# One weight part instead of two is cut between the second gated product and its transposed halves

## The chip, the cores and the metric

The kernel runs on one core of one Trainium2 chip. The metric is the device time of one execution in microseconds, from the first to the last instruction and what lies around them. Of the runs before, the median of three counts.

## What is computed

One decoder layer over 2048 tokens of width 1024: a token mixer with pooling and windowed attention, and then a mixture of experts. The change lies in the experts. Cut to them, the reference is:

```python
def _hier_moe(h, w_group_router, b_group_router, w_expert_router, b_expert_router,
              w_gate, w_up, w_down):
...
    def run_block(args):
        tok, e = args
        xb = h[tok]
        a = xb @ w_gate[e]
        u = xb @ w_up[e]
        return (jax.nn.silu(a) * u) @ w_down[e]

    y = lax.map(run_block, (slot_tok.reshape(n_blocks, MOE_BLOCK), block_expert))
    y = y.reshape(n_slots, D_MODEL) * slot_w[:, None]
    return jnp.zeros((t_count, D_MODEL), h.dtype).at[slot_tok].add(y)
```

Each token goes to 2 of 32 experts; an expert has a gate and an up matrix of 1024x512 and a down matrix of 512x1024, all in float32. The tokens of an expert are padded to blocks of 128.

## The kernel before

The stages follow each other: normalise, project, attend, merge, mix_out, route, experts, combine. The function `experts` runs over blocks of 128 tokens. A row of `table` tells of each block which expert it has, and whether that is a new one. Blocks are sorted by expert; a block whose *next* block has a new expert is called a reload block here. In this case 48 blocks run.

**Precision.** Every float32 matrix is split into a high part (a copy in fp32r) and a low part (the rest): ScalarE makes the high part, VectorE subtracts it to get the low part, and TensorE multiplies three times: high by high, high by low, low by high (`three`, lines 1585 to 1587). To split a part of the weights is called a cut: `cut_high` (L1507, ACT) and `cut_low` (L1513, DVE).

**Weights.** An expert is 12 parts of 512 KB: parts 0 to 3 are the gate and up columns of the first half (256 columns each), 4 to 7 those of the second half, 8 to 11 the down matrix. SyncE loads a raw part (L1214, L1217) when the low cut of the part before it in the same buffer is done (`lo_ready`). There is one raw buffer, and one pair of high and low buffers. So the weights of the next expert are cut within a reload block, each part after its last use in that block (`used[g]`), and the raw parts of the expert behind it are loaded meanwhile.

**A block on TensorE**, in program order: `gate_up(0, 0..3)`, turn (transpose) the gathered tokens of the next block (`turn_x`, L1576), `gate_up(1, 0)`, `gate_up(1, 1)`, turn half 0 of the gated product (`turn_h(0)`), `gate_up(1, 2)`, `gate_up(1, 3)`, `down(0)`, `turn_h(1)`, `down(1)`, wait for `lo_taken[1]`, `down(2)`, `down(3)`. The wait is for the low part of the turned half 1, `moe_hT_lo`. A `down(k)` is six matmuls of 512 columns.

**The same block on ScalarE and VectorE.** ScalarE: `silu(0)` (L1660), high part of the turned tokens (L1639), cuts, high part of turned half 0, cuts, `silu(1)`, cuts, high part of turned half 1 (`take_h(1)`, `moe_hT_hi`), cuts, and last the scaled output (`moe_ys`, L1676). VectorE does the same with `multiply` (L1715), the low parts (L1694) and `cut_low`. The cuts are under a branch that is taken in reload blocks alone. The order on each engine is written out by hand in these functions; each waits for semaphores of the others:

```python
                def take_low(half, dst, hi, n_tiles, count):
                    dve.wait_ge(hi_taken[half], count)
                    dve.tensor_tensor(dst, p_turn[:, half, 0:n_tiles * P], hi, ALU.subtract).then_inc(lo_taken[half], 1)
```

**GpSimd** gathers the tokens of block b+2 (`moe_xg`, L1546) and then adds the output of block b to the sum in memory by an indirect DMA (L1555); the next gather is issued when that scatter has landed.

Of the kernel before, what the change touches and what calls it, by code (L numbers as in the profile page):

```python
# [1223 lines left out]
GU, PARTS = 8, 12  # L1224
# [224 lines left out]
def experts(nc, table, slot_rows, slot_place, slot_share, ident, h_dram, raw_gu, raw_d, w_gate, w_up, w_down, y_sum, x1_dram):  # L1449
# [5 lines left out]
    with ExitStack() as ctx:  # L1455
# [26 lines left out]
        def entry(eng, r, b, top):  # L1482
            return eng.value_load(table[0:1, r, ds(b, 1)], min_val=0, max_val=top)

        def by_twos(eng, body):

            count = entry(eng, 3, 0, NB)
            with eng.Fori(0, NB // 2) as i:
                with eng.If(2 * i < count):
                    body(i)  # L1490
            return count
# [10 lines left out]
        def cut_high(act, g, n, b):  # L1502

            act.wait_ge(part_loaded[g], (32 if g < GU else 16) * n)
            if b is not None:
                act.wait_ge(used[g], b + 1)
            nc.scalar.activation(hi_part(g), raw_part(g), ACT.Copy).then_inc(hi_ready[g], 1)  # L1507

        def cut_low(dve, g, n, b):
            dve.wait_ge(hi_ready[g], n)  # L1510
            if b is not None:
                dve.wait_ge(used[g], b + 1)
            dve.tensor_tensor(lo_part(g), raw_part(g), hi_part(g), ALU.subtract).then_inc(lo_ready[g], 1)  # L1513

        with nc.Block() as block:
            @block.sync
            def _(sp):
                def load(e, before):

                    for g in range(PARTS):  # L1520
                        sp.wait_ge(lo_ready[g], before)
                        load_part(sp, g, e, raw_gu, raw_d, w_gate, w_up, w_down, part_loaded[g])

                for g in range(PARTS):
                    sp.sem_inc(part_loaded[g], 32 if g < GU else 16)  # L1525

                def reload(b):
                    with sp.If(entry(sp, 1, b, 1) > 0):
                        load(entry(sp, 0, b, NE - 1), entry(sp, 2, b, NE))

                by_twos(sp, lambda i: [reload(2 * i), reload(2 * i + 1)])

                cut = entry(sp, 2, NB, NE) + 1
                for g in range(PARTS):
                    sp.wait_ge(lo_ready[g], cut)
                    sp.dma_start(x1_part(g, raw_gu, raw_d), x1_dram[ds(g * P, P), :]).then_inc(x1_loaded, 16)
                sp.wait_ge(x1_loaded, 16 * PARTS)
# [99 lines left out]
            @block.scalar  # L1637
            def _(act):
                copy = lambda dst, src: nc.scalar.activation(dst, src, ACT.Copy)  # L1639

                def take_high(half, dst, n_tiles, count):
                    act.wait_ge(turned[half], count + (4 if half else 0))
                    copy(dst, p_turn[:, half, 0:n_tiles * P]).then_inc(hi_taken[half], 1)

                def take_x(u, count):
                    for half in range(2):
                        take_high(half, xT_hi[:, u, ds(4 * half, 4), :].rearrange("p k c -> p (k c)"), 4, count)

                def block_of(b, u):
                    new = entry(act, 1, b + 1, 1)  # L1650
                    n = entry(act, 2, b + 1, NE) + 1

                    def cuts(parts):
                        with act.If(new > 0):
                            for g in parts:
                                cut_high(act, g, n, b)

                    def silu(half):
                        act.wait_ge(used[4 * half + 3], b + 1)
                        nc.scalar.activation(act_g[:, half, :], p_gu[:, half, 0, 0:H2], ACT.Silu).then_inc(silu_ready[half], 1)  # L1660

                    def take_h(half):
                        take_high(half, hT_hi[:, ds(2 * half, 2), :].rearrange("p k c -> p (k c)"), 2, 2 * b + 3)

                    silu(0)
                    take_x(1 - u, 2 * b + 2)
                    cuts(range(0, 2))
                    take_h(0)
                    cuts(range(2, 3))
                    silu(1)  # L1670
                    cuts(range(3, 5))
                    take_h(1)
                    cuts(range(5, PARTS))
                    act.wait_ge(used[PARTS - 1], b + 1)
                    act.wait_ge(scattered, b + 1)
                    nc.scalar.activation(ys[:, u, :], p_y[:, :, :].rearrange("p a c -> p (a c)"), ACT.Copy,  # L1676
                                         scale=slot_share[:, ds(b, 1)]).then_inc(y_ready, 1)

                for g in range(PARTS):
                    cut_high(act, g, 1, None)  # L1680
                    if g == 1:
                        take_x(0, 1)
                by_twos(act, lambda i: [block_of(2 * i, 0), block_of(2 * i + 1, 1)])

            @block.vector
            def _(dve):
                dve.sem_inc(y_ready, 1)
                for u in range(2):
                    dve.sem_inc(hid_ready[u], 1)
                    dve.sem_inc(lo_taken[u], 1)  # L1690
# [5 lines that stand above are left out]
                def flat(t, k, n):  # L1696
                    return t[:, ds(k, n), :].rearrange("p k c -> p (k c)")

                def take_x(u, count):
                    for half in range(2):  # L1700
                        take_low(half, flat(xT_lo[:, u, :, :], 4 * half, 4), flat(xT_hi[:, u, :, :], 4 * half, 4), 4, count)

                def block_of(b, u):
                    new = entry(dve, 1, b + 1, 1)
                    n = entry(dve, 2, b + 1, NE) + 1

                    def cuts(parts):
                        with dve.If(new > 0):
                            for g in parts:
                                cut_low(dve, g, n, b)  # L1710

                    def multiply(half):
                        dve.wait_ge(silu_ready[half], b + 1)
                        dve.wait_ge(used[4 * half + 3], b + 1)
                        dve.tensor_tensor(hid[:, half, :], p_gu[:, half, 1, 0:H2], act_g[:, half, :], ALU.mult  # L1715
                                          ).then_inc(hid_ready[half], 1)

                    def take_h(half):
                        take_low(half, flat(hT_lo, 2 * half, 2), flat(hT_hi, 2 * half, 2), 2, 2 * b + 3)

                    multiply(0)
                    take_x(1 - u, 2 * b + 2)
                    cuts(range(0, 2))
                    take_h(0)
                    cuts(range(2, 3))
                    multiply(1)
                    cuts(range(3, 5))
                    take_h(1)
                    cuts(range(5, PARTS))

                for g in range(PARTS):
                    cut_low(dve, g, 1, None)
                    if g == 1:
                        take_x(0, 1)
                by_twos(dve, lambda i: [block_of(2 * i, 0), block_of(2 * i + 1, 1)])


# [130 lines left out]
```

## Time and profile before

| | |
|---|---|
| median of 3 runs | 2729.76 us (2728.51 to 2739.48) |
| profiled execution | 2733.67 us, span 2731.9 us, mean granted TensorE clock 0.946 |
| PE busy | 2381.6 us (87%) |
| DVE, ACT, POOL busy | 1338.9, 933.1, 549.2 us |
| blocks run (moe_ys) | 48, from 1767.8 to 2659.9 us |
| loads of an expert | 16 of 256 KB and 4 of 512 KB |

Engines are PE (TensorE; PEld its weight loads), ACT (ScalarE), DVE (VectorE), POOL (GpSimd), SP (SyncE). The expert stage is roughly the stretch from 1752 to 2660 us; the combine stage behind it ends the program. Busy time of PE contains overlapping matmuls: a matmul of 512 columns takes 0.39 us, and one starts each 0.235 us.

### The profile page before, as it was taken

What the parts mean: (1) busy time and instruction counts of PE and PEld (TensorE: products, weight loads), DVE (VectorE), ACT (ScalarE), POOL (GpSimd) and SP (SyncE); (2) the same over time, 40 slices, a digit from 0 to 9 for tenths busy, and PEclk for the clock granted to TensorE, in tenths of its full rate; (3) what the DMA queues carried; (4) which work ended last, traced back from release to release, by engine and by line L of the source; (5) the groups of instructions that cost most, each with busy time, mean ns of one, the idle gap of its engine ahead of it and who ended that gap; (6) DMA issues with size and microseconds to landing.
All of it is one profiled execution on the core that took longest, in us unless ns stands there. A gap on an engine that the chain in (4) does not pass through costs nothing. (4 is left out here: it accounts for less than half of the span.)

```text
span 2731.9 us, 39222 instructions
## 1 busy us (share of the span) xinstructions
PE 2381.6 (87%) x13485; PEld 2039.5 (75%) x13486; DVE 1338.9 (49%) x1673; ACT 933.1 (34%) x1541; POOL 549.2 (20%) x375
## 2 busy tenths in 40 slices
PE   3599999999999968876969995699999999999990
PEld 3488888888888857764857884588898988988880
DVE  7552111123232257636534445888666384655536
ACT  3200000000000035533322221587666375655533
POOL 2311111111111020002334552222222222212220
PEclk9999999999999989957989996799999999999995
DMA  6123222223424233226555444599999597878847
GB/s 231 46 77 123 90 95 98 86 104 111 138 92 138 107 122 119 92 98 216 212 185 195 155 155 153 186 353 356 320 305 284 137 353 231 282 217 279 246 146 292
DMA packets 291435, 493.43 MB, mean 181 GB/s; under 512 B 21145, under 2 KB 226481, under 8 KB 281778
## 3 DMA queue, kind: packets, MB, share of 16 engines
q1 hardware_dynamic: 272658, 424.53, 44.9%
q0 software_dynamic: 14112, 51.39, 8.0%
q10 hardware_dynamic: 4608, 16.78, 1.5%
q8 instruction: 32, 0.52, 0.1%
q14 instruction: 25, 0.20, 0.0%
HBM read 374.98 MB, written 117.64 MB: 180 GB/s over the span
## 5 line engine op out<-in xcount | busy, mean ns | idle before, releaser
L357 PE MATMUL proj_psum<-h_hi,proj_w_hi 128*128 128x512 f32 x1216 | 481.7, 396 | 19.0 <-POOL proj_w_lo L342 19.0
L359 PE MATMUL proj_psum<-h_hi,proj_w_lo 128*128 128x512 f32 x1216 | 481.4, 396 | 0.0
L358 PE MATMUL proj_psum<-h_lo,proj_w_hi 128*128 128x512 f32 x1216 | 481.4, 396 | 0.0
L1585 PE MATMUL moe_p_gu<-moe_hi_gu,moe_xT_hi 128*128 128x256 f32 x1536 | 437.4, 285 | 1.7 <-DVE moe_xT_lo L1694 1.7
L378 DVE COPY proj_out<-proj_psum 128x512 f32<-128x512 f32 x152 | 123.7, 815 | 634.4 <-PE proj_psum L359 633.3
L1586 PE MATMUL moe_p_gu<-moe_lo_gu,moe_xT_hi 128*128 128x256 f32 x1536 | 428.7, 279 | 0.0
L1587 PE MATMUL moe_p_gu<-moe_hi_gu,moe_xT_lo 128*128 128x256 f32 x1536 | 428.6, 279 | 0.0
L1513 DVE TENSOR_TENSOR moe_lo_gu<-raw_gu,moe_hi_gu 128x1024 fp32r<-128x1024 f32 x256 | 302.1, 1220 | 23.5 <-ACT moe_hi_gu L1507 19.4
L335 ACT ACTIVATE proj_w_hi<-proj_raw 128x1024 fp32r<-128x1024 f32 x38 | 40.4, 1062 | 781.5 <-PE proj_psum L359 748.0
L1586 PEld LDWEIGHTS moe_p_gu<-moe_lo_gu,moe_xT_hi 128*128 128x128 f32 x1536 | 291.1, 190 | 2.1
L1585 PEld LDWEIGHTS moe_p_gu<-moe_hi_gu,moe_xT_hi 128*128 128x128 f32 x1536 | 289.2, 188 | 4.2 <-issue 2.1
L1587 PEld LDWEIGHTS moe_p_gu<-moe_hi_gu,moe_xT_lo 128*128 128x128 f32 x1536 | 290.4, 189 | 0.0
L357 PEld LDWEIGHTS proj_psum<-h_hi,proj_w_hi 128*128 128x128 f32 x1216 | 228.8, 188 | 74.6 <-issue 19.3
L359 PEld LDWEIGHTS proj_psum<-h_hi,proj_w_lo 128*128 128x128 f32 x1216 | 228.7, 188 | 55.6
L358 PEld LDWEIGHTS proj_psum<-h_lo,proj_w_hi 128*128 128x128 f32 x1216 | 228.8, 188 | 55.3
L1507 ACT ACTIVATE moe_hi_gu<-raw_gu 128x1024 fp32r<-128x1024 f32 x256 | 256.9, 1056 | 14.3 <-SPq L1525 11.3
L342 POOL TENSOR_TENSOR proj_w_lo<-proj_raw,proj_w_hi 128x1024 fp32r<-128x1024 f32 x38 | 97.8, 2575 | 724.6 <-ACT proj_w_hi L335 724.6
L1585 PE MATMUL moe_p_y<-moe_hi_d,moe_hT_hi 128*128 128x512 f32 x384 | 159.2, 415 | 34.4 <-DVE moe_hT_lo L1694 34.2
L1555 POOL DMA_INDIRECT y_sum<-moe_ys,moe_place x48 | 99.6, 2075 | 345.6 <-ACT moe_ys L1676 334.5
L1715 DVE TENSOR_TENSOR moe_hid<-moe_p_gu,moe_act_g 128x256 f32<-128x256 f32 x96 | 40.7, 424 | 245.8 <-ACT moe_act_g L1660 242.1
L1587 PE MATMUL moe_p_y<-moe_hi_d,moe_hT_lo 128*128 128x512 f32 x384 | 151.9, 396 | 0.0
L1586 PE MATMUL moe_p_y<-moe_lo_d,moe_hT_hi 128*128 128x512 f32 x384 | 151.8, 395 | 0.0
(268 smaller groups left out, 3772.0 us busy)
## 6 DMA issues: line engine op xcount, KB each, us to landing
raw_gu<-in_w_exp_gate SPq DMA_DIRECT2D x256, 256.0 KB, 5.8
raw_gu<-in_w_exp_up SPq DMA_DIRECT2D x256, 256.0 KB, 5.9
raw_d<-in_w_exp_down SPq DMA_DIRECT2D x128, 512.0 KB, 7.9
projected<-proj_out SPq DMA_DIRECT2D x38, 1024.0 KB, 3.9
proj_raw<-in_w_in SPq DMA_DIRECT2D x38, 512.0 KB
att_qkv<-projected SPq DMA_DIRECT2D x18, 1024.0 KB
proj_w_rest<-in_w_ada SPq DMA_DIRECT2D x8, 2048.0 KB
merge_gate<-projected SPq DMA_DIRECT2D x32, 512.0 KB, 5.0
```

The source lines that it names most:

```text
L342: pool.tensor_tensor(w_lo[:, u, :, :], raw[:, u, :, :], w_hi[:, u, :, :], ALU.subtract).then_inc(lo_ready[u], 1)
L357: pe.matmul(bank, w_hi[:, u, k, :], h_hi[:, k, tok], start=(k == 0), stop=False)
L358: pe.matmul(bank, w_hi[:, u, k, :], h_lo[:, k, tok], start=False, stop=False)
L359: mm = pe.matmul(bank, w_lo[:, u, k, :], h_hi[:, k, tok], start=False, stop=(k == KD - 1))
L378: ins = dve.tensor_copy(view[:, ds(tg * per, per), :], psum[:, u, tg, :].rearrange("p (m r) -> p m r", r=dilation))
L1507: nc.scalar.activation(hi_part(g), raw_part(g), ACT.Copy).then_inc(hi_ready[g], 1)
L1513: dve.tensor_tensor(lo_part(g), raw_part(g), hi_part(g), ALU.subtract).then_inc(lo_ready[g], 1)
L1555: pool.indirect_dma_start(out=y_sum, out_offset=bass.IndirectOffsetOnAxis(ap=place[:, u:u + 1], axis=0), in_=ys[:, u, :], in_offset=None, ...
L1585: pe.matmul(bank, x_hi, w_hi, start=first, stop=False)
L1586: pe.matmul(bank, x_hi, w_lo, start=False, stop=False)
L1587: return pe.matmul(bank, x_lo, w_hi, start=False, stop=last)
L1715: dve.tensor_tensor(hid[:, half, :], p_gu[:, half, 1, 0:H2], act_g[:, half, :], ALU.mult).then_inc(hid_ready[half], 1)
```

## The change

On ScalarE and on VectorE, the list of parts that are cut between the second gated product (`silu(1)`, `multiply(1)`) and the copies of its turned half (`take_h(1)`) holds part 3 alone instead of parts 3 and 4. Part 4 is cut first behind those copies. No instruction is added or taken away.

```diff
@@ experts, ACT
                     take_h(0)
                     cuts(range(2, 3))
                     silu(1)
-                    cuts(range(3, 5))
+                    cuts(range(3, 4))
                     take_h(1)
-                    cuts(range(5, PARTS))
+                    cuts(range(4, PARTS))
                     act.wait_ge(used[PARTS - 1], b + 1)
                     act.wait_ge(scattered, b + 1)
@@ experts, DVE
                     take_h(0)
                     cuts(range(2, 3))
                     multiply(1)
-                    cuts(range(3, 5))
+                    cuts(range(3, 4))
                     take_h(1)
-                    cuts(range(5, PARTS))
+                    cuts(range(4, PARTS))
```

On VectorE, in a block's second part, from the branch before the cuts to the end of the block (moe_lo_gu is the low part of gate/up weights, moe_lo_d of down weights, moe_hT_lo of the turned product):

```order
-L1513 TENSOR_TENSOR moe_lo_gu<-raw_gu,moe_hi_gu 128x1024 x2
+L1513 TENSOR_TENSOR moe_lo_gu<-raw_gu,moe_hi_gu 128x1024
 L1708 UNCONDITIONAL_BRANCH
 L1694 TENSOR_TENSOR moe_hT_lo<-moe_p_turn,moe_hT_hi 128x256
 L1708 COMPARE_AND_BRANCH
 L1510 REGISTER_ALU
-L1513 TENSOR_TENSOR moe_lo_gu<-raw_gu,moe_hi_gu 128x1024 x3
+L1513 TENSOR_TENSOR moe_lo_gu<-raw_gu,moe_hi_gu 128x1024 x4
 L1513 TENSOR_TENSOR moe_lo_d<-raw_d,moe_hi_d 128x1024 x4
 L1708 UNCONDITIONAL_BRANCH
```

One low cut has moved from ahead of moe_hT_lo to behind it; the order of the cuts among themselves is the same.

On ScalarE, the same place (moe_hi_gu and moe_hi_d are high parts of the weights, moe_hT_hi of the turned product):

```order
-L1507 ACTIVATE moe_hi_gu<-raw_gu 128x1024 x2
+L1507 ACTIVATE moe_hi_gu<-raw_gu 128x1024
 L1654 UNCONDITIONAL_BRANCH
```

and in the changed kernel from there on:

```order
L1507 ACTIVATE moe_hi_gu<-raw_gu 128x1024
L1654 UNCONDITIONAL_BRANCH
L1642 REGISTER_ALU
L1639 ACTIVATE moe_hT_hi<-moe_p_turn 128x256
L1654 COMPARE_AND_BRANCH
L1504 ISA
L1507 ACTIVATE moe_hi_gu<-raw_gu 128x1024 x4
L1504 REGISTER_ALU
L1507 ACTIVATE moe_hi_d<-raw_d 128x1024 x4
```

One high cut stands ahead of moe_hT_hi and eight behind it, where there were two and seven. TensorE, GpSimd and SyncE have the same instructions in the same order.

## Rows read from the trace of the kernel before

**Rows 1.** Windows: busy us (instructions) of PE, PEld, DVE, ACT, POOL; clock, DMA share, GB/s

```profile
1752.00:1912.00 160.00, 149.16 (x1070) 136.31 (x1069) 136.77 (x147) 126.96 (x158) 35.39 (x29) 1.00 1.07 356
...
2195.00:2253.00 58.00, 54.63 (x394) 50.17 (x393) 50.11 (x54) 47.00 (x59) 13.66 (x13) 1.00 1.07 353
...
1752.00:2660.00 908.00, 868.82 (x6274) 801.66 (x6272) 571.57 (x663) 556.17 (x732) 197.07 (x188) 1.00 0.87 273
```

**Rows 2.** Waits of PE, 1752 to 1928: total us, times, longest

```profile
PE moe_p_y L1585 <- DVE moe_hT_lo L1694: 8.4, 8, 1.1
```

**Rows 3.** Waits of PE, 1928 to 2665

```profile
PE moe_p_y L1585 <- DVE moe_hT_lo L1694: 25.9, 23, 1.1
```

**Rows 4.** The page's groups: busy us, mean ns, idle before

```profile
L1507 ACT ACTIVATE moe_hi_gu<-raw_gu 128x1024 fp32r<-128x1024 f32 x256 | 256.9, 1056 | 14.3 <-SPq L1525 11.3
```

**Rows 5.** Timeline of ACT in a reload block: start us, us, instruction

```profile
2032.23 0.39 ACT L1660 ACTIVATE moe_act_g<-moe_p_gu 128x256 f32<-128x256 f32 x1 [1.50 <-PE moe_p_gu L1587]
2032.51 2.00 ACT L1507 ACTIVATE moe_hi_gu<-raw_gu 128x1024 fp32r<-128x1024 f32 x2
2034.40 0.37 ACT L1639 ACTIVATE moe_hT_hi<-moe_p_turn 128x256 fp32r<-128x256 f32 x1
2034.67 2.95 ACT L1507 ACTIVATE moe_hi_gu<-raw_gu 128x1024 fp32r<-128x1024 f32 x3
```

**Rows 6.** Timeline of DVE in the same block and up to the next

```profile
2025.99 0.42 DVE L1715 TENSOR_TENSOR moe_hid<-moe_p_gu,moe_act_g 128x256 f32<-128x256 f32 x1 [9.23 <-ACT moe_act_g L1660]
...
2032.64 0.42 DVE L1715 TENSOR_TENSOR moe_hid<-moe_p_gu,moe_act_g 128x256 f32<-128x256 f32 x1 [0.65 <-ACT moe_act_g L1660]
2033.59 2.36 DVE L1513 TENSOR_TENSOR moe_lo_gu<-raw_gu,moe_hi_gu 128x1024 fp32r<-128x1024 f32 x2 [0.52 <-ACT moe_hi_gu L1507]
2035.87 0.42 DVE L1694 TENSOR_TENSOR moe_hT_lo<-moe_p_turn,moe_hT_hi 128x256 fp32r<-128x256 f32 x1
2036.20 3.49 DVE L1513 TENSOR_TENSOR moe_lo_gu<-raw_gu,moe_hi_gu 128x1024 fp32r<-128x1024 f32 x3
2039.61 4.62 DVE L1513 TENSOR_TENSOR moe_lo_d<-raw_d,moe_hi_d 128x1024 fp32r<-128x1024 f32 x4
2045.52 0.42 DVE L1715 TENSOR_TENSOR moe_hid<-moe_p_gu,moe_act_g 128x256 f32<-128x256 f32 x1 [1.28 <-ACT moe_act_g L1660]
```

**Rows 7.** Timeline of PE in the same block

```profile
2033.43 0.38 PE L1576 MATMUL moe_p_turn<-ident,moe_hid 128*128 128x128 f32 x2
...
2034.82 0.40 PE L1587 MATMUL moe_p_y<-moe_hi_d,moe_hT_lo 128*128 128x512 f32 x1
2036.34 0.50 PE L1585 MATMUL moe_p_y<-moe_hi_d,moe_hT_hi 128*128 128x512 f32 x1 [1.12 <-DVE moe_hT_lo L1694]
```

**Rows 8.** Waits of ACT, 1752 to 1912

```profile
ACT moe_hi_d L1507 <- DMA raw_d<-in_w_exp_down: 5.5, 13, 1.4
```

**Rows 9.** Timeline of ACT, 1838 to 1849

```profile
1845.70 1.06 ACT L1507 ACTIVATE moe_hi_d<-raw_d 128x1024 fp32r<-128x1024 f32 x1 [0.52 <-DMA raw_d<-in_w_exp_down]
```

**Rows 10.** Timeline of ACT in a block without a reload

```profile
2071.09 0.39 ACT L1660 ACTIVATE moe_act_g<-moe_p_gu 128x256 f32<-128x256 f32 x1 [2.44 <-PE moe_p_gu L1587]
2072.72 0.39 ACT L1639 ACTIVATE moe_hT_hi<-moe_p_turn 128x256 fp32r<-128x256 f32 x1 [1.24 <-PE moe_p_turn L1576]
```

**Rows 11.** Timeline of POOL: two gathers

```profile
1999.32 1.49 POOL L1546 DMA_INDIRECT moe_xg<-h_moe,moe_row  x1 [0.81 <-POOL moe_row L1543]
...
2224.45 1.16 POOL L1546 DMA_INDIRECT moe_xg<-h_moe,moe_row  x1 [0.81 <-POOL moe_row L1543]
```

**Rows 12.** Tile moe_xg, the same two gathers: issue to landing, in this order

```profile
DMA to landing us min/median/max: 7.7/7.7/7.7
...
DMA to landing us min/median/max: 7.3/7.3/7.3
```

**Rows 13.** Timeline of PE: the turns of these two gathers' tokens

```profile
2007.42 1.03 PE L1576 MATMUL moe_p_turn<-ident,moe_xg 128*128 128x128 f32 x8
...
2233.47 1.04 PE L1576 MATMUL moe_p_turn<-ident,moe_xg 128*128 128x128 f32 x8
```

## The prediction

> **What bounds the kernel now.** The change touches only the expert stage, so I first asked which engine sets its pace. In its 908 us TensorE is busy 868.8 us at a granted clock of 1.00, while VectorE has 572 us and ScalarE 556 us [rows 1]. So TensorE is the bound wherever nothing holds it up, and I read next what does. In the lists of TensorE's waits one entry stands out: its down product (moe_p_y) waits for VectorE's low part of the transposed product (moe_hT_lo), 8 times for 8.4 us up to 1928 us [rows 2] and 23 times for 25.9 us after it [rows 3]. That is 31 times 1.1 us, and 31 is the number of reload blocks: 48 blocks run, and 256 high cuts of gate/up parts [rows 4], eight to an expert, are 32 experts, of which the first is cut ahead of the loop. The wait exists only where the cuts stand between, so it belongs to the edited place.
>
> One reload block shows the order. ScalarE starts the second silu at 2032.23, makes two high cuts from 2032.51 and only then copies the transposed high part at 2034.40 [rows 5]. VectorE starts its two low cuts at 2033.59 and hT_lo at 2035.87 [rows 6]. TensorE has ended the two transposes at 2033.81, runs the last matmul of down(1) from 2034.82 and starts down(2) at 2036.34, idle for 1.12 us [rows 7]. The reader is to see that the transposes were done well ahead of both copies: what is late is VectorE.
>
> The second thing to see is the DMA. From 1752 to 1912 us, eight reload blocks in a row, the DMA share is 1.07 at 356 GB/s; it is the same in 2195 to 2253, and 0.87 over the stage [rows 1]. In the first run ScalarE waits 13 times for a down part to land [rows 8], for the first time at 1845.70, in the fifth block [rows 9]; after 1912 us its list has no such wait.
>
> **The change part by part.** Nothing is added: 12 high and 12 low cuts per reload block stay. Part 4 moves behind the copy of the transposed half 1.
>
> *VectorE.* Two low cuts and the step to hT_lo take 2035.87 - 2033.59 = 2.28 us [rows 6], so 1.14 each. With one cut, hT_lo may start at 2034.73 if its high part is there. That copy needs the transposes' end at 2033.81 [rows 7]; counted from the second silu, a block without cuts has it at 2072.72 - 2071.09 = 1.63 us [rows 10], here 2033.86, while the one high cut left ends at about 2033.5. The copy takes 0.37 and ends at 2034.25, 0.5 us before VectorE asks. So VectorE's part 3 remains the last to end, and the gain is one cut, 1.14 us.
>
> *TensorE.* It started down(2) 0.47 us behind hT_lo's start, so now at 2035.20. Its own pace is 0.235 per matmul, so it was free at 2034.82 + 0.235 = 2035.06 [rows 7]. A wait of 0.14 us is left; it could at most have won 1.28. Gain: 1.14 per reload block.
>
> *What moves later.* ScalarE now stands idle from 2033.5 to 2033.86 in front of the transposes, with all remaining cuts queued behind. Part 5 was cut from 2034.67 [rows 5]; now part 4 starts at about 2034.13 and part 5 at 2035.1, 0.4 us later. On VectorE part 4 starts at about 2035.2 and part 5 at 2036.35, against 2036.20 [rows 6]: 0.15 later. VectorE ends its last cut (started in the group at 2039.61, 4 x 1.14) near 2044.4 instead of 2044.23, and is wanted for the next multiply at 2045.52 - 1.14 = 2044.38 [rows 6]. So its idle 1.28 us shrinks to nothing, just without a loss. ScalarE keeps about 1 us. A few tenths late there are covered: turn_h(0) comes only after two more gate/up parts. If the cover were gone, the 0.15 to 0.4 us per block would be paid.
>
> *Loads.* SyncE issues a raw part once its low cut is done. An expert is 6.29 MB, a gather and a scatter 0.52 MB each: 7.34 MB per reload block, at 355 GB/s (between the two runs' rates) 20.7 us. A reload block has 2045.52 - 2025.99 = 19.5 us, of which the row at 2045.52 is the second end. The DMA already needs more than the blocks give it. In the first run the lead is used up, and its end is set by the landings: what TensorE wins there it loses again. So for the 8 blocks ahead of 1928 us I take 0, from bounds of 0 and 8 x 1.14 = 9.1 us. Later runs are at most four blocks; the deficit grows from 1.2 to 2.3 us per block. The first run lost its lead, some 5 us, within five blocks [rows 9]; three intervals now cost 6.9, so the last block of the two runs of four could see its down parts up to 1.9 us late, mostly hidden by ScalarE's slack: 0 taken, 3.8 as a bound.
>
> *Gathers.* A gather is issued only when the scatter of three blocks before has landed, which does not move with the stall of the block between. The gather at 1999.32 landed 7.7 us later, at 2007.0 [rows 11, 12], and its tokens were turned at 2007.42 [rows 13]: 0.4 us of slack against 1.14. This one costs 0.7. The one at 2224.45 landed at 2231.75 and was wanted at 2233.47: 1.7 of slack, 0.6 left. VectorE's cuts show 11 places after 1928 us where two reload blocks follow each other, and so 11 gathers of this kind. I let 2 of the other 10 slip like the first (0.9 each): 0.7 + 1.8 = 2.5 us; bounds 0.7 and 0.7 + 9.
>
> The DMA limit is where a page speaks. The row shows 356 GB/s at a share of 1.07 with ScalarE waiting for landings. The Trainium skill, page "DMA: Bandwidth & Descriptors", section "Measured (HBM→SBUF, 128 partitions, SWDGE, issued from GpSimd)", has 425 GB/s for a core whose neighbour is idle. By that figure an expert's block would need 17.3 us, no run would be held, and the first rival below would be right. The trace does not agree: at a full share it moves 356 over 160 us, and I go by the row.
>
> **Sum.** 23 x 1.14 = 26.2, less 2.5, is 23.7 us. The profiled execution took 2733.67 us with a span of 2731.9; it becomes 2710.0. The median of the runs is 2729.76, 0.14% below it, and becomes 2706.1. I predict 2706. What follows the experts starts with the last block's end and moves as a whole.
>
> **The rivals.**
> *Full gain in all 31 blocks.* If the first run were paced by TensorE after all, 31 x 1.14 = 35.3 us go: 2694.4. For it: that run's first four blocks show no landing wait. Against: the 13 waits behind them [rows 8]. 7%.
> *The DMA takes more.* All 10 close gathers slip by 0.9 and both runs of four end 1.9 late: 26.2 - 9.7 - 3.8 = 12.7 us gained, 2717. For it: the share of 1.07 in 2195 to 2253 already now [rows 1], and gathers pass through the same engines. Against: four later blocks with it show no wait for a landing. 14%.
> *No change.* VectorE is so full that the next multiply and x copies are late by what was won, or the wait merely turns into one for the next x: about 2730. For it: 1.28 us of idle time against 1.14 + 0.15. Against: it still waits 0.65 us for the second silu [rows 6], which takes up a few tenths just ahead of the place that matters. 8%.
> *Slower.* ScalarE's stand in front of the transposes becomes the pace: cuts, low cuts and reloads all come 0.4 us later per reload block, and TensorE waits for the parts instead: 31 x 0.4 = 12.4 us, 2742. It decides where the transposes end more than 0.5 us after part 3's high cut and VectorE has no idle time left. Against: they end 0.3 after it. 3%.
> My forecast has the remaining 68%, with a range of its own of 2700 to 2712.
>
> **The numbers.** About 0.5%, 13.6 us, is what a measurement here tells from no change, so "faster" begins under 2716.1. The forecast, the full gain and nearly half of the DMA rival lie there: 0.68 + 0.07 + 0.07 = 0.82; slower by over 0.5% (above 2743.4) is half of its rival and stray cases: 0.03; the same 0.15. The range is 2698 to 2718: it takes in the forecast and nearly all of the DMA rival, and leaves out the full gain, no change and slower.
>
> **What would show it.** TensorE's wait for moe_hT_lo falls from 1.1 to 0.1 to 0.2 us, the start of down(2) stands 0.47 behind hT_lo; ScalarE idles about 0.3 before that copy. Blocks with a reload take 18.4 us instead of 19.5, those without stay at 17.9. Before 1928 us nothing is won and ScalarE waits longer for raw_d. New waits of TensorE for moe_xg appear, the first near 2007. VectorE's idle time before the multiply after a reload block is close to 0. The prediction is wrong if the first run also gets shorter, if waits for moe_xg come in most runs, or if ScalarE's waits for landings appear after 1928 us.

## The result and the profile after

The changed kernel took 2716.05 us (median of 6 runs, 2713.35 to 2722.47); the kernel before 2733.89 (6 runs, 2728.51 to 2739.48). The ratio is 0.9937, interval 0.992 to 0.9955: 17 us faster, between 12 and 22. The prediction had 23.7 us less and 2706; its range, 2698 to 2718, holds the time near its upper end. Of the 10 us between 2706 and 2716, 4 are there because the forecast counted from 2729.76, the median of three runs of the kernel before, and all six have 2733.89; the other 6 are a smaller gain. One execution of all those below, at 3167.91 us and a granted clock of 0.728 beside 0.93 to 0.95 in the others, is left out of every median and ratio.

The profiled execution took 2717.12 us, its span is 2715.4. The same block as in [rows 5 to 7], a reload block after one without, in the timeline of the changed kernel; TensorE first:

```profile
2033.27 0.38 PE L1576 MATMUL moe_p_turn<-ident,moe_hid 128*128 128x128 f32 x2
...
2034.65 0.40 PE L1587 MATMUL moe_p_y<-moe_hi_d,moe_hT_lo 128*128 128x512 f32 x1
2035.04 0.50 PE L1585 MATMUL moe_p_y<-moe_hi_d,moe_hT_hi 128*128 128x512 f32 x1
```

ScalarE:

```profile
2025.39 0.38 ACT L1660 ACTIVATE moe_act_g<-moe_p_gu 128x256 f32<-128x256 f32 x1 [2.30 <-PE moe_p_gu L1587]
...
2032.06 0.38 ACT L1660 ACTIVATE moe_act_g<-moe_p_gu 128x256 f32<-128x256 f32 x1 [1.50 <-PE moe_p_gu L1587]
2032.34 1.05 ACT L1507 ACTIVATE moe_hi_gu<-raw_gu 128x1024 fp32r<-128x1024 f32 x1
2033.68 0.38 ACT L1639 ACTIVATE moe_hT_hi<-moe_p_turn 128x256 fp32r<-128x256 f32 x1 [0.29 <-PE moe_p_turn L1576]
2033.96 3.89 ACT L1507 ACTIVATE moe_hi_gu<-raw_gu 128x1024 fp32r<-128x1024 f32 x4
2037.75 3.89 ACT L1507 ACTIVATE moe_hi_d<-raw_d 128x1024 fp32r<-128x1024 f32 x4
2041.55 1.10 ACT L1676 ACTIVATE moe_ys<-moe_p_y,slot_share 128x1024 f32<-128x1024 f32 x1
```

VectorE:

```profile
2033.42 1.23 DVE L1513 TENSOR_TENSOR moe_lo_gu<-raw_gu,moe_hi_gu 128x1024 fp32r<-128x1024 f32 x1 [0.52 <-ACT moe_hi_gu L1507]
2034.57 0.42 DVE L1694 TENSOR_TENSOR moe_hT_lo<-moe_p_turn,moe_hT_hi 128x256 fp32r<-128x256 f32 x1
2035.05 4.63 DVE L1513 TENSOR_TENSOR moe_lo_gu<-raw_gu,moe_hi_gu 128x1024 fp32r<-128x1024 f32 x4
2039.60 4.62 DVE L1513 TENSOR_TENSOR moe_lo_d<-raw_d,moe_hi_d 128x1024 fp32r<-128x1024 f32 x4
2044.14 0.41 DVE L1715 TENSOR_TENSOR moe_hid<-moe_p_gu,moe_act_g 128x256 f32<-128x256 f32 x1
```

The step between the two matmuls of TensorE is 0.39 us, where it was 1.52. hT_lo starts 2.51 us behind the second silu instead of 3.64, ScalarE stands 0.29 us in front of the transposes, and the next multiply follows VectorE's last cut without idle time. So far each row is as foreseen, but for 0.1 us: the multiply starts 0.54 us behind its silu at 2043.60, where it was 0.42. Now what TensorE waits for, in two lists of its waits, 1752 to 1930 and 1930 to 2650 us, which answer to [rows 2, 3]:

```profile
PE moe_p_turn L1576 <- DMA moe_xg<-h_moe,moe_row: 6.6, 5, 2.0
PE moe_p_turn L1576 <- DVE moe_xT_lo L1694: 4.2, 3, 2.1
PE moe_p_y L1585 <- DVE moe_hT_lo L1694: 0.3, 1, 0.3
```

```profile
PE moe_p_turn L1576 <- DMA moe_xg<-h_moe,moe_row: 9.2, 10, 1.9
```

The wait for moe_hT_lo is gone, and one for the gathered tokens, moe_xg, has come: 9.2 us behind the first run, in place of 25.9. Nine of its ten waits, 8.4 us, stand in the 11 places where two reload blocks have just followed each other; the tenth, 0.8 us, is in the tenth block, where the kernel before waited 1.3. Reading the same two marks in every trace, the first silu of the tenth block and the last moe_ys, gives the table that the experiments below are read by. "First run" is from the first silu to the tenth block's, "rest" from there to the start of the last moe_ys; both in us. The stage begins at another time in each trace (1737.7 to 1764.6), by differences ahead of it; the two stretches leave that out, and what lies behind them takes 71.8 to 72.4 us in all.

| kernel | first run | rest | both |
|---|---|---|---|
| before | 175.2 | 731.7 | 907.0 |
| changed | 176.4 | 713.4 | 889.8 |
| VectorE's list alone | 175.7 | 713.8 | 889.6 |
| ScalarE's list alone | 177.5 | 742.3 | 919.8 |
| changed, gather ahead | 177.2 | 704.4 | 881.6 |
| before, gather ahead | 176.2 | 729.6 | 905.8 |
| before, half loads | 173.3 | 730.9 | 904.2 |
| changed, half loads | 163.4 | 703.9 | 867.3 |
| changed, moe_ys early | 175.9 | 701.7 | 877.6 |
| before, moe_ys early | 177.2 | 729.8 | 907.0 |
| no part between | 176.5 | 728.2 | 904.7 |
| changed, both cures | 176.4 | 702.6 | 879.0 |

Each row is one execution. The change won 18.3 us in the rest and lost 1.2 in the first run; the three versions of the kernel before with full loads have 175.2 to 177.2 there, so 1.2 is no more than they differ among themselves.

### The profile page after: what moved, and what is told of

Read it like the earlier page. It is cut to its first block and busy times, and to the rows that moved or that the text cites. A ratio compares the mean times of both kernels' runs of the same rounds, so it can differ in the third digit from the quotient of the medians.

```text
span 2715.4 us, 39222 instructions
## 1 busy us (share of the span) xinstructions
PE 2385.7 (88%) x13485; PEld 2043.5 (75%) x13486; DVE 1337.3 (49%) x1673; ACT 935.4 (34%) x1541; POOL 534.0 (20%) x375
## 5 line engine op out<-in xcount | busy, mean ns | idle before, releaser
L1555 POOL DMA_INDIRECT y_sum<-moe_ys,moe_place x48 | 93.0, 1937 | 343.5 <-ACT moe_ys L1676 330.9
L1513 DVE TENSOR_TENSOR moe_lo_d<-raw_d,moe_hi_d 128x1024 fp32r<-128x1024 f32 x128 | 148.8, 1217 | 4.6 <-ACT moe_hi_d L1507 4.2
```

The lines of the kernel that those rows point to most:

```text
L1555: pool.indirect_dma_start(out=y_sum, out_offset=bass.IndirectOffsetOnAxis(ap=place[:, u:u + 1], axis=0), in_=ys[:, u, :], in_offset=None, ...
```

## Why the gathers came due

My theory after the result: a gather is released by the landing of the scatter three blocks before, that scatter by moe_ys, and moe_ys stands on ScalarE behind the cuts. TensorE's gain did not move moe_ys forward within its block at all. In the block shown it starts 2041.55 - 2025.39 = 16.16 us behind the first silu. Before it was

```profile
2041.30 1.11 ACT L1676 ACTIVATE moe_ys<-moe_p_y,slot_share 128x1024 f32<-128x1024 f32 x1
```

(timeline of ACT), 15.73 us behind the silu at 2025.57. So it became 0.43 us later within the block, while TensorE became 1.14 earlier in this block and again in the next. One close gather of the changed kernel, from ScalarE's timeline, GpSimd's and TensorE's:

```profile
2188.75 1.10 ACT L1676 ACTIVATE moe_ys<-moe_p_y,slot_share 128x1024 f32<-128x1024 f32 x1
...
2190.67 2.22 POOL L1555 DMA_INDIRECT y_sum<-moe_ys,moe_place  x1 [11.61 <-ACT moe_ys L1676]
2200.75 0.97 POOL L1543 COPY moe_row<-slot_rows 128x1 int32 x1 [7.85 <-DMA y_sum<-moe_ys,moe_place]
2202.51 1.17 POOL L1546 DMA_INDIRECT moe_xg<-h_moe,moe_row  x1 [0.80 <-POOL moe_row L1543]
...
2208.87 0.28 PE L1587 MATMUL moe_p_gu<-moe_hi_gu,moe_xT_lo 128*128 128x256 f32 x1
2209.78 0.66 PE L1576 MATMUL moe_p_turn<-ident,moe_xg 128*128 128x128 f32 x4 [0.62 <-DMA moe_xg<-h_moe,moe_row]
```

From moe_ys to the turn there are 21.0 us, of which the chain takes all. The reader should follow the brackets backwards: TensorE waits for the gather, the gather's row copy for the scatter's landing, the scatter for moe_ys. The rivals were that VectorE, now full, takes the time, and that the loads do.

## The experiments

Each ratio is to executions of the kernel before that lie beside those of the experiment. Their median is 2732.74 us for the lists of one engine and the gathers, 2737.43 for the half loads, the early output on the changed kernel and no part between, and 2737.49 for the two that remain. So across these groups only ratios and the two stretches are compared, not times.

**One engine's list alone.** Each leaves the other engine as before.

```diff
 # VectorE alone: block_of of the vector engine
-                    cuts(range(3, 5))
+                    cuts(range(3, 4))
                     take_h(1)
-                    cuts(range(5, PARTS))
+                    cuts(range(4, PARTS))
```

> Only VectorE's list is changed (part 3 alone ahead of moe_hT_lo); ScalarE keeps parts 3 and 4 ahead of moe_hT_hi. Theory (the won time is lost at gathers, which hang on the scaled output moe_ys; moe_ys is queued on ScalarE behind the cuts and came 0.4 us later with the change): TensorE's wait for moe_hT_lo goes as it did with the change (0.1 to 0.2 us left), moe_ys stays at 15.75 us behind the block's first silu instead of 16.15, and TensorE's waits for moe_xg after 1930 us fall from 9.2 us to 4 to 6. Time 3 to 5 us below the changed kernel's, ratio to before 0.992 to 0.993. Rival (VectorE is full, its late multiply costs the time): waits and time as with the change, ratio 0.9937.

Measured: 2717.2 us, ratio 0.9943 (0.9925 to 0.9961). The gain is VectorE's, as both theories had it. The further 3 to 5 us did not come, and this expectation missed: moe_ys did return to 15.7 us, but the waits fell only to 7.5 us, not to 4 to 6:

```profile
PE moe_p_turn L1576 <- DMA moe_xg<-h_moe,moe_row: 7.5, 10, 1.0
```

The scatter of the same block as above, in GpSimd's timeline, shows where the 0.4 us went:

```profile
2190.22 2.55 POOL L1555 DMA_INDIRECT y_sum<-moe_ys,moe_place  x1 [11.21 <-ACT moe_ys L1676]
2200.76 1.12 POOL L1543 COPY moe_row<-slot_rows 128x1 int32 x1 [7.99 <-DMA y_sum<-moe_ys,moe_place]
```

It is issued 0.45 us earlier, takes 2.55 instead of 2.22 us and has landed at the same time. A shift this small doesn't tell the theories apart.

> Only ScalarE's list is changed; VectorE keeps parts 3 and 4 ahead of moe_hT_lo. Theory: VectorE's second low cut is what holds TensorE, so the wait of 1.1 us stays in all 31 reload blocks, while moe_ys comes about 0.4 us later: ratio 1.000 to 1.002. Rival (ScalarE's high cut is what is late): the wait falls to under 0.5 us and the ratio to 0.995.

Measured: 2747.33 us, ratio 1.0056 (1.0038 to 1.0074), 15 us slower than before. I had missed that VectorE's second low cut needs the high cut of the same part, and that this now stands behind the wait for the transposes. ScalarE, then VectorE, in a reload block:

```profile
2034.44 0.38 ACT L1660 ACTIVATE moe_act_g<-moe_p_gu 128x256 f32<-128x256 f32 x1 [1.50 <-PE moe_p_gu L1587]
...
2036.34 3.89 ACT L1507 ACTIVATE moe_hi_gu<-raw_gu 128x1024 fp32r<-128x1024 f32 x4
...
2037.43 1.22 DVE L1513 TENSOR_TENSOR moe_lo_gu<-raw_gu,moe_hi_gu 128x1024 fp32r<-128x1024 f32 x1 [0.40 <-ACT moe_hi_gu L1507]
2038.57 0.42 DVE L1694 TENSOR_TENSOR moe_hT_lo<-moe_p_turn,moe_hT_hi 128x256 fp32r<-128x256 f32 x1
```

hT_lo starts 4.13 us behind the silu instead of 3.64. TensorE's 23 waits in the rest are 37.1 us, 1.6 each, against 25.9. TensorE has no wait for the gathers in this stretch; its reload blocks are slower than before.

**The gather ahead of the scatter's landing**, on the changed kernel and on the one before. Besides what is shown, the row table and its zeroed tail get two more columns, as gathers now run one block further ahead.

```diff
...
+                def landed(b):
                     pool.wait_ge(added, 16 * b + 16)
                     pool.sem_inc(scattered, 1)
 
                 def block_of(b, u):
-                    gather(b + 2, u)
                     scatter(b, u)
+                    gather(b + 3, 1 - u)
+                    landed(b)
...
                 gather(1, 1)
+                gather(2, 0)
```

> The changed kernel, with GpSimd issuing the gather for block b+3 right behind the scatter of block b instead of after that scatter has landed (its own wait for the landing comes behind the gather). Theory: no wait of TensorE for moe_xg is left after 1930 us (9.2 us now), so reload blocks there take 18.4 us each and 23 x 1.14 = 26 us are won against before in that stretch, while the first run up to 1930 us stays held by the loads: 2706 to 2709, ratio 0.990 to 0.991. Rival (the loads or VectorE take the time and the gathers' waits only stand where another would): the waits move elsewhere and the ratio stays 0.993 to 0.994.

> The kernel before with the same earlier gathers, as the control. Theory: its gathers had 0.4 us of slack or more except two (2.1 us of waits), so 0 to 2 us are won: ratio 0.999 to 1.000. Rival (gathers behind the scatters were a cost of the kernel before as well): ratio 0.996 or less.

Measured: the changed kernel with it 2710.76 us, ratio 0.9928 (0.99 to 0.9955); the one before with it 2730.65, ratio 0.9993 (0.9983 to 1.0003). The ratio is above the 0.990 to 0.991 expected and hardly below the rival's 0.993, and the four times lie between 2703.62 and 2716.62, which is more than the effect. By the times alone nothing is decided; the traces decide: the rest is 704.4 us against 713.4, and the list of TensorE's waits in it is empty. Against before that is 27.3 us. In the kernel before, the same edit brought 2.1 us in the rest. The first run did not get shorter with either.

**Half of the bytes of each reload**, before and changed. The other half of each raw part keeps the first expert's values, so these two kernels do not compute the reference's result; they serve to see what the loads cost.

```diff
+            eng.dma_start(raw_gu[:, g, m, 0, :], w[0, ds(e, 1), ds(kp * 2 * P, P), ds(half * H2, H2)]
+                          .rearrange("e p f -> p (e f)")).then_inc(loaded, 16)
...
+        eng.dma_start(raw_d[:, g - GU, 0:D // 2], w_down[0, ds(e, 1), ds((g - GU) * P, P), 0:D // 2].rearrange("e p f -> p (e f)")
```

> The kernel before, with each reload of an expert's part fetching only half of its bytes (one of two row groups of gate/up, half the columns of down); the rest of the raw part keeps the first expert's values, so what the experts compute is not the reference's. Theory: the loads bound the kernel before only at the end of its first run of reload blocks, so little changes: first run up to the tenth block about 1 us shorter, the rest 0 to 2 us; ratio 0.998 to 1.000. Rival (loads slow the whole stage through the DMA engines): ratio under 0.995.

> The changed kernel with the same halved reloads (the same part of the computation altered). Theory: with the DMA engines at little more than half their load neither landings nor gathers hold the blocks, so all 31 reload blocks keep the 1.14 us: 35 us against the halved kernel before, 2695 to 2699, ratio to before 0.986 to 0.988; first run about 9 us shorter than before's 175.2. Rival A (the first run is held by something else): the first run stays at 175 to 176 us, ratio 0.990. Rival B (VectorE is full and takes part of it): waits on neither, yet the reload blocks take 18.8 us or more.

Measured: 2729.19 us, ratio 0.9973 (0.9954 to 0.9992), and 2690.68, ratio 0.9835 (0.9815 to 0.9855): 38.5 us between the two. The kernel before hardly noticed the halved loads, 1.9 us in the first run and 0.8 in the rest. The changed one did: its first run fell from 176.4 to 163.4 us, 9.9 below the halved kernel before. All 31 blocks now keep what they won: 904.2 - 867.3 = 36.9 us in the two stretches. ScalarE's waits in the first run say what it was. In the changed kernel they were

```profile
ACT moe_hi_d L1507 <- DMA raw_d<-in_w_exp_down: 7.5, 16, 1.3
...
ACT moe_hi_gu L1507 <- DMA raw_gu<-in_w_exp_up: 4.7, 8, 1.3
```

and with half loads neither is in the list. The windows of 160 us over the first run, changed kernel and then half loads:

```profile
1752.00:1912.00 160.00, 150.97 (x1073) 137.81 (x1072) 137.11 (x147) 126.68 (x157) 28.86 (x28) 0.99 1.07 356
```

```profile
1765.00:1925.00 160.00, 158.73 (x1141) 145.52 (x1140) 137.50 (x152) 127.75 (x162) 36.97 (x33) 1.00 0.78 216
```

TensorE is busy for 158.7 of 160 us once the DMA share is 0.78. It is also seen that VectorE, with as much work as ever (137.1 and 137.5 us), was not what held the blocks. The edit takes both effects away at once: the landing of a gather, 7.1 us in the median in the kernel before, is 5.1 here, and no wait for moe_xg is left in the rest. As issuing the gather earlier removes the same wait with the loads whole, the wait needs both, the late issue and the loads beside it.

**moe_ys ahead of the last three high cuts**, on the changed kernel and on the one before.

```diff
-                    cuts(range(4, PARTS))
+                    cuts(range(4, 9))
                     act.wait_ge(used[PARTS - 1], b + 1)
                     act.wait_ge(scattered, b + 1)
                     nc.scalar.activation(ys[:, u, :], ...
+                    cuts(range(9, PARTS))
```

> The changed kernel, with ScalarE's scaled output moe_ys put ahead of the last three high cuts instead of behind them (it comes 2.5 to 3 us earlier in the block). Theory (the gathers hang on moe_ys through the landing of the scatter): TensorE's waits for moe_xg after 1930 us fall from 9.2 us to under 2, and the stretch behind the first run takes 705 to 707 us instead of 713.4: 2708 to 2710, ratio 0.991. Rival (the scatter's landing is set by the loads queued in the DMA engines, not by its issue): the waits stay at 6 to 9 us and the ratio at 0.994.

> The kernel before (two parts ahead of the transposed halves), with moe_ys ahead of the last three high cuts. Control for the last run but one: if the gathers had slack before, the earlier output wins next to nothing there: PE's waits for moe_hT_lo stay at 34 us, the stretch behind the first run at 729 to 731 us, ratio 0.998 to 1.000. Rival (the earlier output helps by itself, whatever the gathers): ratio 0.995 or less.

Measured: 2703.08 us, ratio 0.9887 (0.9865 to 0.991), on the changed kernel, and 2735.85, ratio 1.0 (0.9983 to 1.0017), on the one before. ScalarE's timeline shows the output between the cuts of the down parts:

```profile
2030.24 1.05 ACT L1507 ACTIVATE moe_hi_d<-raw_d 128x1024 fp32r<-128x1024 f32 x1
2031.19 1.10 ACT L1676 ACTIVATE moe_ys<-moe_p_y,slot_share 128x1024 f32<-128x1024 f32 x1
2032.19 2.95 ACT L1507 ACTIVATE moe_hi_d<-raw_d 128x1024 fp32r<-128x1024 f32 x3
```

With the output 2.9 us earlier, the list of TensorE's waits in the rest is empty, and the rest is 701.7 us, 3 us below what was expected. The loads and GpSimd's own order are as in the changed kernel, so the late output is what released the gathers late. This is the fastest version with whole loads: 1.1% below before, and by the ratios 0.5% below the changed kernel. The same edit without the change wins nothing: the gathers had slack there.

**No part between**, on both engines.

```diff
-                    cuts(range(3, 4))
                     take_h(1)
-                    cuts(range(4, PARTS))
+                    cuts(range(3, PARTS))
```

> No part at all is cut between the second gated product and its transposed halves, on both engines. Theory: the last 0.15 us of TensorE's wait for moe_hT_lo goes, but VectorE then stands idle until the high part is there and has 1.0 us of cuts more behind it than there is room for; its multiply and copies come late in runs of reload blocks and moe_ys about 1 us later still, so the gathers' waits grow to 15 to 20 us: 2720 to 2730, ratio 0.995 to 0.999. Rival (the cuts behind are hidden): ratio 0.992 to 0.994.

Measured: 2731.24 us, ratio 0.9986 (0.997 to 1.0002), 1 us over the time foreseen, within the ratio. The rest of the stage is 728.2 us. TensorE's waits in 1925 to 2700, then ScalarE and VectorE around the end of a reload block that another one precedes:

```profile
PE moe_p_turn L1576 <- DMA moe_xg<-h_moe,moe_row: 20.2, 9, 2.5
```

```profile
2057.99 1.09 ACT L1675 ACTIVATE moe_ys<-moe_p_y,slot_share 128x1024 f32<-128x1024 f32 x1
2059.10 1.28 ACT L1660 ACT_TABLE_LOAD   x1
2060.39 0.38 ACT L1660 ACTIVATE moe_act_g<-moe_p_gu 128x256 f32<-128x256 f32 x1
```

```profile
2050.54 5.77 DVE L1513 TENSOR_TENSOR moe_lo_gu<-raw_gu,moe_hi_gu 128x1024 fp32r<-128x1024 f32 x5 [0.53 <-ACT moe_hi_gu L1507]
2056.22 4.62 DVE L1513 TENSOR_TENSOR moe_lo_d<-raw_d,moe_hi_d 128x1024 fp32r<-128x1024 f32 x4
2060.81 0.42 DVE L1714 TENSOR_TENSOR moe_hid<-moe_p_gu,moe_act_g 128x256 f32<-128x256 f32 x1
```

The multiply starts 0.42 us behind its silu in a free block, and here too, 2060.81 with a silu at 2060.39: VectorE is not what is late, because the silu is late too, behind moe_ys and the load of a function table (ACT_TABLE_LOAD, 1.28 us). One part between is thus the best of the three as the rest of the kernel stands: with two VectorE holds TensorE, with none ScalarE's output and the gathers do. No part between together with the early output was not tried.

**Both cures together.**

> The changed kernel with both cures, the gather ahead of the scatter's landing and moe_ys ahead of the last three high cuts. Theory: both remove the same waits, so together they give what one gives: no wait for moe_xg, the stretch behind the first run at 701 to 705 us, the first run held by the loads at 175 to 177 us; ratio 0.988 to 0.990. Rival (the two cure different losses): the stretch falls below 700 us, ratio 0.986 or less.

Measured: 2707.42 us, the median of three runs (2702.9 to 2714.63), ratio 0.9892 (0.9844 to 0.9941). The rest is 702.6 us, beside 704.4 and 701.7 with one cure. They remove the same waits.

## Why the prediction was right, and where it was off

The wait, the size of what it gives back and the hold of the loads on the first run were foreseen for the right reasons. The loss to the gathers was named, but priced at a quarter of what it was. By one of its own signs the prediction was wrong there: it said so of waits for moe_xg that come in most runs, and they come in all seven runs of two or more reload blocks behind the first run. The first of them is at 1968.5, not near 2007. The first half of the rival *The DMA takes more*, ten close gathers late by 0.9 us each, at 14%, is much nearer to what happened than the forecast's three. That the range still held the time is in part its width: the 17.2 us won in the two stretches lie between the forecast's 23.7 and that rival's 12.7.

- *The wait and its size.* Right. 31 waits of 1.1 us went; hT_lo moved by 1.13 us, and 0.15 us of standstill is left, where 0.14 was worked out. ScalarE alone (slower) and VectorE alone (the whole gain) show that VectorE's second cut held TensorE.
- *ScalarE 0.4, VectorE 0.15 us later.* Right in size: part 5's low cut starts 4.13 us behind the silu where it was 3.97 (2035.05 + 1.14 - 2032.06, and [rows 5, 6]), and ScalarE's cuts end 0.41 later. That the next multiply just fits was right to 0.1 us. What was wrong is that the prediction followed only the cuts behind them, and not the instruction that ends ScalarE's list, moe_ys.
- *The first run wins nothing.* Right: 1.2 us more where 9.1 fewer were at stake; the halved loads show that it was the loads. With the gather ahead TensorE's waits for moe_xg are gone from the first run too, and it is no shorter. The DMA moved 356 GB/s over these 160 us in the changed kernel as in the one before. The figure of 425 GB/s that the prediction quotes from the Trainium skill, page "DMA: Bandwidth & Descriptors", section "Measured (HBM→SBUF, 128 partitions, SWDGE, issued from GpSimd)", was not reached here.
- *The gathers.* The mechanism was right and the size was not. The step "which does not move with the stall of the block between" put the fall in slack at 1.14 us. It is 2.7: before, 22.9 us lay between the moe_ys at 2210.54 (ScalarE's timeline) and the turn at 2233.47 [rows 13]; in the changed kernel the turn would be due at 2209.0, 20.2 us behind the moe_ys at 2188.75. Over the 11 places it is 22.9 to 23.1 before, and 20.0 to 20.5 in the nine where the changed kernel waits. moe_ys was never paced by TensorE in a reload block (it waits for TensorE 17 times in either trace, the number of blocks without a reload), so both blocks' 1.14 count, and its own 0.43 comes on top. So not 3 of 11 close gathers were late but 9, at 0.9 us each. The other two stand in the last block of a run of four, and there the turn one block earlier had itself been late by 0.9 and 0.6 us.
- *The sum.* 23.7 was foreseen; the two stretches gave 17.2, the span 16.5. Taking the starts of TensorE's matmuls in the rest, from each to the next, the steps of the down products are 26.1 us shorter than before, where 23 x 1.14 gives 26.2, and those that lead to or within the turns 9.9 us longer. (The list shows less, as it counts idle time from the modelled end of the matmul ahead.) So the term of 2.5 was 9.9, outside its own upper bound of 9.7. The steps within the gate/up matmuls are 2.1 us shorter, which nothing in the prediction foresaw: 26.1 - 9.9 + 2.1 = 18.3 us. The difference of 6.5 is then 7.4 for the gathers and 1.2 for the first run, less those 2.1, which are luck.
- *The DMA rival's second half*, down parts late at the ends of the runs of four, was not seen behind 1930 us: ScalarE has no wait for a landing there. It shows with the gather ahead, nine waits of ScalarE and 2.2 us in all, at no cost to TensorE.
- *Not settled:* with the gather ahead the rest won 27.3 us, as 23 x 1.14 + 1.3 = 27.5 says (1.3 is the tenth block's wait for moe_xg), and with the early output 30.0. The traces say where 2.5 of the 2.7 more lie: in the steps of the gate/up matmuls. The 48 that open a block take, from the first start to the last, either 5.33 or 5.54 us, both at a granted clock of 1.00. The longer time stands in 19 of the 38 blocks behind the tenth in the kernel before, in 8 in the changed one, in 20 with the gather ahead and in 8 with the early output. Over the twelve traces 174 of its 175 cases fall where VectorE was cutting meanwhile; but 102 blocks with such cuts have the shorter time, so what decides is open.

## What to carry to other kernels

When one engine gets ahead, look at each loop that leads back to it through other queues, and ask where its start is anchored. An instruction that another engine sets, here the output at the end of ScalarE's list, does not come along; the slack then falls by the gain of every block that the loop spans, and by what the anchor itself slips. And an item that releases a long transfer is best put ahead of work that nobody waits for: here the two stretches won 29.4 us with the early output and 17.2 without it, and the early output alone won nothing.

## What was not expected of the hardware

The landing of a scatter with addition to memory took 10.0 us in the median of the kernel before and 7.5 with half loads; a gather's 7.1 and 4.5. So about 2.5 us of either went with half of the weight loads. GpSimd's scatter instruction itself took between 1.60 and 2.49 us, and its copy of one column of 128 int32 0.19 to 1.28 us in the kernel before; both stand in the chain that released TensorE. What lengthens them was not tried. The same 48 gate/up matmuls took 5.33 or 5.54 us at one granted clock, the longer time almost only while VectorE was cutting.
